# The first half of block u0 moved ahead of the sample tile's turn and the parameters' turn

## The reference

```python
xn = _rmsnorm(x, g_mix)
proj = xn @ w_in                       # 1024 x 3072: u_s 512, u_p 512, gate_s 1024, gate_p 1024
abar, bbar = _ssm_discretise(a_re, a_im, log_dt, b_re, b_im)     # small: 32 groups x 64 states
o_s, hr, hi = _ssm_branch(u_s, h_re, h_im, abar, bbar, c_re, c_im, d, w_glu_a, w_glu_b)
o_p, nh = _pool_branch(u_p, hist, start, pool_w, pool_scale)
x = x + (sigmoid(gate_s) * o_s + sigmoid(gate_p) * o_p) @ w_out
x = _hmoe(x, g_ffn, routers, w_gate, w_up, w_down)   # 32 experts of width 512, each token uses 2
y = _rmsnorm(x, g_final)
```

## Time and profile before

| what | value |
|---|---|
| median of 3 runs | 890.25 us (890.24 to 891.76) |
| the profiled execution's own time | 890.11 us |
| its span | 888.5 us |
| TensorE busy | 800.5 us (90%) |
| TensorE weight load busy | 450.1 us (51%) |
| VectorE busy | 262.2 us (30%) |
| HBM traffic over the span | 291 GB/s |

### The profile page before, as it was taken

One profiled execution on the slowest core, in us unless ns is written; L12 is line 12 of the kernel. 1 busy time (PEld: TensorE's weight loads), 2 busy tenths in 40 slices (PEclk: granted clock), 3 DMA queues, 4 the chain that ended last, 5 costly groups with the idle time before them and its releaser, 6 DMA issues.

```text
span 888.5 us, 9599 instructions
## 1 busy us (share of the span) xinstructions
PE 800.5 (90%) x3864; PEld 450.1 (51%) x3865; DVE 262.2 (30%) x734; ACT 120.4 (14%) x228; POOL 128.1 (14%) x224
## 2 busy tenths in 40 slices
PE   4999999999999899989999789779778877979876
PEld 4888888778888655543333233333223332323222
DVE  5899558320011245552111011011101101111115
ACT  5010021120000133310000000000000000000012
POOL 3000007850123300010111010010001001000000
PEclk9999999999999999999999898889899989989999
DMA  8522022253200393378999999999999999999966
GB/s 294 160 96 95 9 99 56 94 178 141 95 1 0 130 428 159 124 301 305 429 425 428 428 424 428 426 428 424 426 428 426 428 428 424 428 424 405 415 241 249
DMA packets 44688, 251.59 MB, mean 283 GB/s; under 512 B 13397, under 2 KB 14249, under 8 KB 32194
## 3 DMA queue, kind: packets, MB, share of 16 engines
q1 hardware_dynamic: 37682, 237.57, 65.9%
q0 software_dynamic: 6672, 12.86, 4.0%
q10 hardware_dynamic: 288, 0.53, 0.2%
HBM read 245.33 MB, written 13.46 MB: 291 GB/s over the span
## 4 chain that ended last, share of the span: by engine, by line
PE 64%; DMA 29%; SPq 4%; issue 1%; DVE 1%; ACT 1%; POOLq 0%; ACTq 0%; DVEq 0%
PE ps L1417 26%; DMA arena<-in_w_exp_up 25%; PE ps L1686 14%; PE ps L1701 7%; PE ps L1563 6%; SPq L438 3%; PE ps L1773 2%; DMA x_rows<-arena 1%; PE ps L1502 1%; PE ps L1497 1%; DMA arena<-in_x_prompt 1%; PE ps L1676 1%; PE ps L1551 1%; PE ps L1693 1%; PE ps L1585 1%
## 5 line engine op out<-in xcount | busy, mean ns | idle before, releaser
L1686 PE MATMUL ps<-arena 128*64 128x512 f32 x1024 | 250.8, 645 | 56.4 <-DMA arena<-in_w_exp_up 56.2
L1417 PE MATMUL ps<-arena 128*128 128x272 f32 x1024 | 237.3, 393 | 0.1
L1417 PEld LDWEIGHTS ps<-arena 128*128 128x128 f32 x1024 | 194.0, 190 | 39.8 <-ACT arena L648 0.2
L1686 PEld LDWEIGHTS ps<-arena 128*64 128x64 f32 x1024 | 82.5, 148 | 202.3 <-issue 194.0
L1701 PE MATMUL ps<-arena 128*64 128x512 f32 x512 | 116.4, 595 | 2.0 <-DVE arena L1333 2.0
L1337 DVE TENSOR_SCALAR arena<-ps,arena 128x512 f32<-128x512 f32 x32 | 24.0, 751 | 198.4 <-PE ps L1701 198.4
L814 DVE TENSOR_TENSOR arena<-arena 128x256 f32<-128x256 f32 (+11 forms) x217 | 74.6, 344 | 11.1 <-ACT arena L723 3.9
L1302 DVE TENSOR_TENSOR arena<-ps,arena 128x1024 f32<-128x1024 f32 x15 | 18.4, 1225 | 180.3 <-PE ps L1676 180.3
L1701 PEld LDWEIGHTS ps<-arena 128*64 128x64 f32 x512 | 37.3, 137 | 65.5 <-issue 61.3
L580 POOL DMA_INDIRECT y_parts<-arena x32 | 31.9, 998 | 237.1 <-DVE arena L1337 237.1
L764 ACT ACTIVATE arena<-ps,arena 128x512 f32<-128x512 f32 x32 | 22.0, 687 | 308.5 <-PE ps L1686 308.5
(11 more groups left out here) (227 smaller groups left out, 491.9 us busy)
## 6 DMA issues: line engine op xcount, KB each, us to landing
arena<-in_w_exp_gate SPq DMA_DIRECT2D x29, 2048.0 KB, 42.3
arena<-in_w_exp_up SPq DMA_DIRECT2D x29, 2048.0 KB, 31.8
arena<-in_w_exp_down SPq DMA_DIRECT2D x29, 2048.0 KB, 37.4
arena<-in_w_in SPq DMA_DIRECT2D x6, 2048.0 KB, 9.0
arena<-in_w_exp_gate SPq DMA_DIRECT2D x12, 512.0 KB, 13.0
arena<-in_w_exp_up SPq DMA_DIRECT2D x12, 512.0 KB, 19.2
arena<-in_w_exp_down SPq DMA_DIRECT2D x6, 1024.0 KB, 19.0
arena<-in_x_prompt SPq DMA_DIRECT2D x8, 512.0 KB, 6.3
```

What stands on the lines that cost most here:

```text
L1417: last = pe.matmul(dst[:, hh, 0:HALF], w[:, k, m * P:(m + 1) * P], rhs[:, k, hh * HALF:(hh + 1) * HALF], start=(k == 0), stop=(k == kk - 1))
L1686: last = pe.matmul(ps[n * TILE:(n + 1) * TILE, 2 + par, :], x_t[:, k, :], w[:, k, :], start=(k == 0), stop=(k == KD - 1))
```

## The change

Before, TensorE turned all five token tiles, then the parameters, waited for the copy of the sample tile, and ran the whole of u0. Now it turns the four prompt tiles, waits for weight piece 0 and for the copy of tile 2, runs the first half of u0 (tokens 0 to 271, which need only tiles 0 to 2), and then turns the sample tile and the parameters, waits for the sample tile's copy, and runs the second half. The same matmuls are done; none is added.

```diff
             pe.wait_ge(consts, 1)
-            for i in range(TT):
+            def turn_tile(i):
                 dst, r = begin(f"xt{i}"), ROWS[i]
                 pe.wait_ge(xn_ready, i + 1)
...
+            def half_project(dst, w, m, hh):
+                for k in range(KD):
+                    last = pe.matmul(dst[:, hh, 0:HALF], w[:, k, m * P:(m + 1) * P],
+                                     xn_t[:, k, hh * HALF:(hh + 1) * HALF], start=(k == 0), stop=(k == KD - 1))
+                return last
...
+            for i in range(4):
+                turn_tile(i)
+            w = arrived(0)
+            u_0 = begin("u0")
+            pe.wait_ge(emptied["act"], emptied_by("act", NUM["xt2"]))
+            half_project(u_0, w, 0, 0)
+            turn_tile(4)
             pe.wait_ge(small_in, 16 * 9)
             pe.wait_ge(dt_ready, 2)
             dst = begin("par")
...
-            w = arrived(0)
-            project("u0", w, xn_t, 0, KD)
+            end(half_project(u_0, w, 0, 1))
             pe.wait_ge(c_loaded, 16 * 8)
             dst = begin("ct")
```

More of the change, by code:

```diff
@@ L1402, in _, with arrived @@
                 end(last)
+            def half_project(dst, w, m, hh):
[3 more added lines that the diff above has]
+                return last
+            def arrived(b):
+                pe.wait_ge(w_stream[b % 3], 16 * (b // 3 + 1))
+                return w_slot(b % 3, 4 if b in (6, 7) else 8)
+            for i in range(4):
[5 more added lines that the diff above has]
+            turn_tile(4)
             pe.wait_ge(small_in, 16 * 9)
@@ L1419, in project @@
                 end(last)
-            def arrived(b):
-                pe.wait_ge(w_stream[b % 3], 16 * (b // 3 + 1))
-                return w_slot(b % 3, 4 if b in (6, 7) else 8)
-            w = arrived(0)
-            project("u0", w, xn_t, 0, KD)
+            end(half_project(u_0, w, 0, 1))
             pe.wait_ge(c_loaded, 16 * 8)
```

## The result

The changed kernel is slower: ratio 1.0033 to the kernel before, with a 95% interval of 1.0021 to 1.0045, from 20 runs of each. Of 892.1 us that is 2.9 us (1.9 to 4.0). The medians are 895.51 us (892.19 to 897.77) and 892.09 (890.24 to 896.86), 3.4 us apart. The three runs shown first are among these 20 of the kernel before, and they were fast ones: seven of the 20 lie at 890.2 to 890.7, the other 13 at 891.4 to 896.9. The profiled execution of the changed kernel took 894.0 us, its span is 892.4, 3.9 us more than before.

What follows compares the result with a forecast made beforehand. TensorE's list was taken to bound the mixer, the weight stream the experts. Gain 0.46 us, less 0.20, less about 1.7 at gs0, made 1.45 us slower: 891.70 from the median, said as 891.6, range 889.9 to 893.3.

Steps and rivals of the forecast that it cites:

- TensorE's clock: At gs0: a pause of 1.8 us could halve the clock afterwards, 3.0 us on top of 1.45, giving 894.7; chance 5%.
- the sum: Whole kernel: gain 0.46 us, less 0.20, less about 1.7 of wait at gs0, is -1.45 us; said 891.6, chance 67%.
- the release of VectorE: Behind the moved half: the parameters reach VectorE 3.6 us later, at 23.6 for 19.97 us.
- the base: Whole kernel before the change: the runs' median, 890.25 us, 0.14 above the profiled execution's 890.11.
- the slack at gs0: At gs0, which reuses ct's PSUM pair: slack of 2.0 us, a 3.6 us delay, so TensorE waits 1.7 to 1.9.
- When the first half can start: First half of u0 on TensorE: starts at about 18.41 us, tile 3 being the last thing it needs.
- The margin that I gave it: Weight piece 0 before the first half: 0.5 to 0.9 us in hand; chance of its being late 8%.
- The clock at the start: TensorE's start: granted clock 1.00 from 13.3 us on behind transposes alone, so the moved half runs at full clock.
- this rival: Moved half behind transposes alone: by the skill's rule at half clock, 3.7 us more, 895.3; no chance of its own given.
- What would show it: Trace signs: half from about 18.4 us, parameters' copy about 23.5, ct about 51.3, gs0 pause 1.7, `kt` wait near 5.4.
- The last sign: Mixer's end: the last gated block ends about 1.45 us later than 299.78, and the whole kernel is later too.

Runs made afterwards that it cites:

- the control with ScalarE's ct: The kernel before, with ScalarE instead of VectorE emptying ct; ratio to before 1.0000 (0.9984 to 1.0016).
- the two warmed kernels with the split: The changed kernel with unread products, 24 at the start and twelve in the pause behind the mixer; ct emptied by VectorE or ScalarE: medians 893.44 and 890.60 us.
- the warmed kernel before: The kernel before, with 24 unread products at the start and twelve in the pause behind the mixer; median 891.01 us, ratio to before 0.9973.

## Why the prediction was wrong

The range was 889.9 to 893.3 and the time is 895.5. The way the change acts on the mixer was foreseen. The step that failed is TensorE's clock, which the sum put at nothing; two further sizes, the release of VectorE and the base, were off. By an estimate from the figures below, the 3.9 us that were missing are 1.8 for the base, 0.5 for the mixer (1.9 for 1.45) and 1.35 for the clock.

*What bounds the kernel, and the slack at gs0.* This was right. VectorE's chain from the parameters to ct took 51.90 - 24.12 = 27.78 us for the 27.75 of the sum, and TensorE waited 1.67 us for the 1.7 to 1.9. Taking ct from VectorE removes the mixer's loss, moving the parameters alone brings nearly all of it.

*When the first half can start.* 18.41 was said, 18.60 measured. Tile 3's turns took 1.57 us for 1.42. Weight piece 0 took 10.0 us to land in the one trace that I had; in the changed kernel it took 10.9, in all other traces 10.0 to 11.1 (12.4 in the control with ScalarE's ct). In the changed kernel it so came at 18.5, and in the two warmed kernels with the split, at 18.4, it was what the half waited for. The margin that I gave it came from one trace.

*The release of VectorE.* This is the term of the sum that was mis-sized: +3.6 said, +4.15 in the profile, +3.5 to +3.9 in the four other traces. The parts in the profile are 0.19 from the start, 0.19 from the half itself (3.86 us for 3.67, at half clock for its first loads), and 0.36 of idle behind the half where I had put 0.20. With 0.1 more for the signal and 0.03 in VectorE's chain, gs0's first matmul came at 52.05, 2.14 us later for the +1.45 of the sum, and the mixer's end 2.22. The mean over five traces, +1.9, is nearer.

*TensorE's clock, the rival with 5%.* This is the step that failed. I priced a fall of the clock behind gs0's wait, at 3.0 us, and read the 1.00 of the stretches as evidence that none would come. Nothing fell at gs0: the 13 records behind its wait took 3.22 us, 0.25 each, where half clock took 0.43 (8 records in the 3.40 us from 20.00 on in the warmed kernel before). But the mixer's end has a pause too, the clock does fall behind it, and I had ruled that out by the earlier trace rows, one execution of a thing that varies. In the profile of the changed kernel it costs 1.69 us, the rest of the 3.9. The Trainium skill (TensorE: Matmul & The Clock Gate, Part 1) says that when the clock moves depends on the run; the five traces of the kernel before agree, one with the fall and four without.

*The clock at the start.* I wrote that the clock was 1.00 from 13.3 us on, behind transposes alone. That was a misreading: the durations show half clock (1.57 us for eight turns, 0.85 when warmed) under a printed 1.00. What the Trainium skill (TensorE: Matmul & The Clock Gate, Part 1) says of a slow start agrees with the trace. What the Trainium skill says of transposes (Part 4 of the same page, not Part 1) does not: in the kernel before, the turns of the sample tile (0.57 us for eight loads of 32 rows, the same in the warmed kernels, and 0.92 where the clock was late) already ran at full clock with nothing but turns ahead of them. So the moved half was not at half clock throughout; it took 3.86 us, 0.19 more than said and not 3.7 more. That the 895.3 of this rival is near the measured 895.5 is chance.

*The base.* I took 890.25 as the kernel's time. It is the time of its fastest executions; the median of 20 is 892.09. That alone puts 1.8 us between forecast and result, about as much as the clock, and the spread that I gave the sum was too narrow for the same reason. With the base at 892.09 the same sum gives 893.5, still 2.0 us below the result.

*What would show it.* The half project without a wait, ct at 51.3 (51.90), the pause before gs0, `kt` at 5.4 (5.58) all came. The last sign, a mixer later by 1.45 and a kernel by as much, did not.

## What to carry to other kernels

When work is pulled forward into a small gap, look at what it pushes back and who starts from that: here 0.46 us of idle were to be won on TensorE, and the push of 4 us met a slack of 2 us at a PSUM pair that another engine empties at the end of a long chain. A step that only starts another engine's chain belongs first in the list, and a buffer that TensorE needs back should not be emptied from the end of such a chain. And a clock that falls behind some pauses, in a kernel whose executions spread by 7 us, makes single traces poor evidence of times: compare the place of an event over several traces, and take the base from more than three runs. Filling the pause took the half clock out of all six traces in which it was tried.

## What the runs showed of the hardware

The printed granted clock says 1.00 for the first 17 to 19 us of these executions, while TensorE's turns took twice as long as in a warmed one (0.20 and 0.11 us a load). In the control with ScalarE's ct it says 1.00 at 22 to 24 us too, under loads of 0.36 us for 0.22. Durations of equal instructions are the better witness there.

In that control u0 began at half clock at 21.98 us, and the mixer ended at 303.2 for 299.8. Of these 3.4 us, 1.2 are the token tile that came late; the other 2.2 are, by an estimate from the loads' durations, the late rise of the clock. One such execution costs the mixer more than the change does.

A pause of 2.87 us behind the mixer was followed by half clock in eight of 14 traces, and in none of the six in which twelve small products filled it. Half clock there cost 1.3 to 1.7 us on a product of 3.66.

Behind 272-column matmuls, the first weight load of a 32-row tile came after 0.36 us of idle in the loads, while the 128-row turns of ct let their first load go right behind (27.51 and 27.55 in the changed kernel). With the parameters alone behind the half, the 100-row load went right behind (22.93 and 22.98), and the 15-row loads came after 0.26 us of idle.
